# Attention of two transformer layers: score maxima in 512-key parts, the row of maxima by VectorE transposes, three or four score banks, and VectorE rounding four tiles per GQA head

## The reference, cut to what matters

```
def gqa_attend(q, k, v):
    s = jnp.einsum('bqhgd,bkhd->bhgqk', q, k).astype(jnp.float32) * (GQA_HEAD_DIM ** -0.5)
    p = jax.nn.softmax(s, axis=-1).astype(v.dtype)
    return jnp.einsum('bhgqk,bkhd->bqhgd', p, v)

def mla_attend(q_nope, q_rope, k_nope, k_rope, v):
    s = (jnp.einsum('bqhd,bkhd->bhqk', q_nope, k_nope)
         + jnp.einsum('bqhr,bkr->bhqk', q_rope, k_rope)).astype(jnp.float32) * ((MLA_NOPE + MLA_ROPE) ** -0.5)
    p = jax.nn.softmax(s, axis=-1).astype(v.dtype)
    return jnp.einsum('bhqk,bkhd->bqhd', p, v)
```

## Time and profile before

| | us |
|---|---|
| three runs | 3592.72, 3584.24, 3588.08 |
| median | 3588.08 |
| the profiled execution | 3586.85 |
| its span in the trace | 3585.0 |
| PE busy in it | 3351.6 (93%) |
| DVE, ACT, POOL busy | 2186.5, 1793.4, 1535.2 |
| GQA attention | about 1820 to 2382 |
| MLA attention | about 2919 to 3487 |

### The profile page before, as it was taken

The page is one execution under the profiler, slowest core; times in us unless marked ns, Lnnn a source line. Parts: engine busy times, 40 slices in busy tenths (PEclk is TensorE's granted clock), DMA queues, the critical chain, the costliest instruction groups (busy, mean ns, idle before and its releaser), DMA issues.

```text
span 3585.0 us, 47856 instructions
## 1 busy us (share of the span) xinstructions
PE 3351.6 (93%) x14934; PEld 2655.1 (74%) x14934; DVE 2186.5 (61%) x2655; ACT 1793.4 (50%) x3060; POOL 1535.2 (43%) x977
## 2 busy tenths in 40 slices
PE   7999999999999999799889999989888989999999
PEld 5777877778888887587777777767765667777767
DVE  6674877477575757447246666666558865555551
ACT  3343868242010101434158888861465657887870
POOL 3303444434444444510156666656210026666652
PEclk9999999999999999899999999999999989999999
DMA  2134232311212121123433443412254344332311
GB/s 99 53 117 119 75 77 81 119 41 66 75 59 88 55 86 35 58 102 115 124 89 66 102 85 76 103 64 89 97 197 149 118 118 111 65 82 53 76 42 71
DMA packets 196086, 313.52 MB, mean 87 GB/s; under 512 B 100928, under 2 KB 111680, under 8 KB 195968
## 3 DMA queue, kind: packets, MB, share of 16 engines
q1 hardware_dynamic: 195968, 312.01, 29.8%
HBM read 234.02 MB, written 77.92 MB: 87 GB/s over the span
## 4 chain that ended last, share of the span: by engine, by line
PE 68%; DVE 12%; issue 7%; ACT 6%; POOL 3%; DMA 2%; SPq 2%; DVEq 0%; ACTq 0%; POOLq 0%
PE PBX L281 10%; PE PBX L283 10%; PE PBX L282 10%; PE PMX L281 5%; PE PMX L282 5%; PE PMX L283 5%; PE PMX L1952 4%; PE PD L1993 2%; PE PD L1994 2%; PE PD L1995 2%; PE PD L856 2%; DVE gqa_m L2083 1%; PE PBX L1977 1%; PE PBX L1976 1%; PE PBX L1978 1%
## 5 line engine op out<-in xcount | busy, mean ns | idle before, releaser
L216 POOL TENSOR_TENSOR w_hi<-w_stage,zero 128x1024 fp32r<-128x1024 f32 (+2 forms) x123 | 229.1, 1863 | 1263.4 <-PE PBX L283 789.3
L2061 POOL TENSOR_TENSOR gqa_pl<-gqa_pf,gqa_ph 128x512 fp32r<-128x512 f32 (+1 forms) x288 | 370.9, 1305 | 186.3 <-ACT gqa_ph L2034 185.7
L2061 POOL TENSOR_TENSOR mla_pl<-mla_pf,mla_ph 128x512 fp32r<-128x512 f32 x256 | 351.8, 1383 | 206.9 <-ACT mla_ph L2034 202.7
L2083 DVE TENSOR_REDUCE gqa_m<-PMX 128x1 f32<-128x1280 f32 (+1 forms) x158 | 200.9, 1271 | 173.6 <-PE PMX L1952 172.7
L218 POOL TENSOR_TENSOR w_lo<-w_stage,w_hi 128x1024 fp32r<-128x1024 f32 (+2 forms) x123 | 299.9, 2438 | 9.7
L1678 ACT ACTIVATE conv_in<-PBX 128x512 f32<-128x512 f32 x66 | 39.6, 601 | 480.6 <-PE PBX L283 476.6
L2083 DVE TENSOR_REDUCE mla_m<-PMX 128x1 f32<-128x1280 f32 x126 | 187.3, 1487 | 89.5 <-PE PMX L1952 88.9
L2029 ACT ACTIVATE mla_pf<-PBX 128x512 f32<-128x512 f32 x320 | 190.1, 594 | 98.0 <-PE PBX L1978 88.1
L2029 ACT ACTIVATE gqa_pf<-PBX 128x512 f32<-128x512 f32 (+1 forms) x352 | 202.1, 574 | 52.8 <-PE PBX L1981 48.6
L2034 ACT ACTIVATE gqa_ph<-gqa_pf 128x512 fp32r<-128x512 f32 (+1 forms) x352 | 215.6, 612 | 13.8
L281 PE MATMUL PBX<-ffn_hi,w_hi 128*128 128x512 f32 x528 | 207.5, 393 | 8.5 <-DVE ffn_lo L653 8.5
(11 more groups left out here) (411 smaller groups left out, 9915.1 us busy)
## 6 DMA issues: line engine op xcount, KB each, us to landing
mod_w<-in_w_mod SPq DMA_DIRECT2D x48, 512.0 KB, 3.5
w_stage<-in_w_up SPq DMA_DIRECT2D x44, 512.0 KB, 3.4
w_stage<-in_w_go SPq DMA_DIRECT2D x24, 512.0 KB, 3.8
gqa_k<-kh_d SPq DMA_DIRECT2D x32, 320.0 KB, 4.9
gqa_q<-qh_d SPq DMA_DIRECT2D x32, 320.0 KB, 7.7
w_stage<-in_w_down SPq DMA_DIRECT2D x24, 384.0 KB, 3.0
qh_d<-heads_qh SPq DMA_DIRECT2D x32, 256.0 KB, 2.0
ql_d<-heads_ql SPq DMA_DIRECT2D x32, 256.0 KB, 2.3
```

Of the source, the lines that this page charges most:

```text
L216: pool.tensor_tensor(w_hi[s][:, 0:st.cols], w_stage[s][:, 0:st.cols], z, ALU.add).then_inc(w_hi_done, 1)
L2061: eng.tensor_tensor(self.PL[k % 4][:, 0:n], self.PF[k % 4][:, 0:n], self.PH[k % 4][:, 0:n].bitcast(F32), ALU.subtract).then_inc(self.lo_dv ...
L2083: dve.tensor_reduce(self.M[g % 2][:, t:t + 1], MX[:, 0:w], AX.X, ALU.max, negate=True)\
```

## The change

All of it is in `Attention`.

- Maxima are made in parts of at most 512 keys: three parts (512, 512, 256) for each tile, each in one bank, in two banks in turn. DVE reduces each part by itself into `m`, a table of 4 tiles by 3 parts.
- The row is made by DVE alone: a reduction over the parts with the sign turned, into column 0 of each 32 of `neg`, four 32 by 32 block transposes into `row`, and a copy of one row into Q. `diag`, `bcast` and ACT's row copy go.
- Score banks: three in GQA, four in MLA, for two. `pf`, `ph` and `pl` have rings of six (GQA) and five (MLA), for four. Three output banks in GQA, one per chunk, for two.
- `LAG` is 4, for 3; on DVE `final` stands two further steps behind.
- The two key blocks of a context chunk share one bank and are one step, so a GQA head has 21 steps.
- In the four GQA steps whose subtraction is DVE's, DVE also rounds `pf` to `ph`, which ACT did.
- The plan: parts go one to a step and two to a step in turn, and the next head's first maxima stand in step 11 of a GQA head and in step 10 of an MLA head. The first tile of chunk 1 is made in the head before.

```
-            LAG = 3
+            LAG = 4
-                self.S = [PB[0], PB[1]]
-                self.BC = PB[2]
-                self.O = [PD[0], PD[1]]
+                self.S = [PB[0], PB[1], PB[2]] + [PMX[:, 2 * C:3 * C]] * self.mla
+                self.NS, self.NP = len(self.S), len(self.PF)
+                self.O = [PD[0], PD[1], PMX[:, 2 * C:3 * C]][:len(chunks)]
+                self.MX = [PMX[:, 0:C], PMX[:, C:2 * C]]
+                self.groups = [[(t,) for t in keys[c]] if len(keys[c]) > 2 else [tuple(keys[c])]
+                               for c in range(len(chunks))]
...
                 else:
-                    plan += [(12 + 2 * t, "max", (1, 0), t) for t in range(4)] + [(21, "bcast", (1, 0), 0)]
+                    plan += [u for t in range(4) for u in tile((11 + 2 * t, 12 + 2 * t, 12 + 2 * t), (1, 0), t)]
+                    plan += tile((19, 20, 20), (1, 1), 0)
+                self.dve_hi = lambda k: not self.mla and self.dve_lo(k)
...
     (sp)
-                    sp.wait_ge(self.pv, i * self.SB + CR_PV2)
+                    sp.wait_ge(self.pv, i * self.SB + self.NP)
...
     (pe)
+                    lo, hi = self.part_keys(c, part)
+                    pe.matmul(MX[unit % len(MX)][:, 0:hi - lo], self.Q[q][0][0:mr, o:o + P], self.K[q][0][0:mr, lo:hi],
+                              start=True, stop=True).then_inc(self.max, 1)
-                    pe.matmul(self.BC[:, 0:n], ones[:, :], self.D[g % 2][:, 0:n // P, :], start=True, stop=True)\
-                      .then_inc(self.bcast, 1)
...
     (act)
-                    act.activation(dst, self.BC[r:r + 1, 0:n], ACT.Copy).then_inc(self.row_done, 1)
+                    if self.dve_hi(k):
+                        return
...
     (low)
+                if self.dve_hi(k):
+                    eng.wait_ge(self.pv, i * self.SB + (k + 1))
+                    eng.wait_ge(self.exp, i * self.SB + (k + self.NS + 1))
+                    eng.tensor_copy(self.PH[k % self.NP][:, :], self.PF[k % self.NP][:, :]).then_inc(self.hi_dve, 1)
...
     (dve)
+                    dve.tensor_reduce(NEG[:, 0:m, 0], M[:, 0:m, 0:parts], AX.X, ALU.max, negate=True).then_inc(self.neg, 1)
+                    for b in range(4):
+                        dve.transpose(blocks[:, :, b, :], NEG[32 * b:32 * b + 32, 0:m, :]).then_inc(self.turned, 1)
+                    dve.tensor_copy(self.Q[q][0 if self.mla else 1][r:r + 1, o:o + n], self.ROW[r:r + 1, 0:n])                       .then_inc(self.row_done, 1)
```

More of the change, by code:

```diff
@@ L1821, in __init__, with tile @@
+                self.steps = [(q, c, g, x == 0, x == len(self.groups[c]) - 1) for q in range(2)
+                              for c in range(len(chunks)) for x, g in enumerate(self.groups[c])]
                 self.SB = len(self.steps)
                 self.NC = len(chunks)
+                def tile(steps, at, t):
+                    return [(steps[p], at, t, p) for p in range(3)]
                 if self.mla:
-                    plan = [(2 * t, "max", (0, 1), t) for t in range(4)] + [(8, "bcast", (0, 1), 0)]
@@ new lines, in __init__ @@
+                    plan += [u for t in range(4) for u in tile((10 + 2 * t, 11 + 2 * t, 11 + 2 * t), (1, 0), t)]
+                    plan += tile((18, 19, 19), (1, 1), 0)
+                else:
+                    plan = [u for t in range(1, 4) for u in tile((2 * t - 2, 2 * t - 1, 2 * t - 1), (0, 1), t)]
+                    plan += [(7 + t, (0, 2), t, 0) for t in range(2)]
+                    plan += [u for t in range(4) for u in tile((11 + 2 * t, 12 + 2 * t, 12 + 2 * t), (1, 0), t)]
+                    plan += tile((19, 20, 20), (1, 1), 0)
@@ L1982, in scores @@
                     mm.then_inc(self.scores, 1)
                 def values(i, k):
-                    q, c, t, first, last_ = self.steps[k]
+                    q, c, tiles, first, last_ = self.steps[k]
                     n = self.chunks[c][1]
@@ L2045, in rden @@
+                    act.activation(rd, self.O[c][64:128, 0:n], ACT.Ln).then_inc(self.rden, 1)
                     act.wait_ge(self.rden, i * (4 * NC) + (2 * x + 1))
-                    act.activation(self.RD[:, 0:n], self.RD[:, 0:n], ACT.Exp, scale=-1.0).then_inc(self.rden, 1)
-                row(0, 0, 0, 0)
-                def step(i, k, last):
-                    for kind, q, c, t, g, tile, over in self.tasks(k, last):
-                        if kind == "bcast":
-                            row(i, q, c, g)
-                    probs(i, k)
@@ L2055, in act @@
-                self.run(act, step, lambda i, k: rden(i, k) if self.steps[k][4] else None)
-            def low(self, eng, i, k):
-                n = self.chunks[self.steps[k][1]][1]
-                eng.wait_ge(self.hi, i * self.SB + (k + 1))
-                eng.tensor_tensor(self.PL[k % 4][:, 0:n], self.PF[k % 4][:, 0:n], self.PH[k % 4][:, 0:n].bitcast(F32),
+                    act.activation(rd, rd, ACT.Exp, scale=-1.0).then_inc(self.rden, 1)
+                self.run(act, lambda i, k, last: probs(i, k), lambda i, k: rden(i, k) if self.steps[k][4] else None)
@@ L2086, in diag @@
[L2086 to L2093 removed]
+                dve.memset(self.NEG[:, :, :], 0.0).then_inc(self.neg, 1)
```

224 lines of the change are left out of this document (109 added, 115 removed).

## The result

| | before | changed |
|---|---|---|
| median | 3586.35 | 3751.54 |
| range of the runs | 3584.24 to 3592.72 | 3741.12 to 3756.14 |
| span of the profiled execution | 3585.0 | 3747.4 |
| granted clock of PE, mean | 0.977 | 0.957 |

The ratio is 1.0453, 95% interval 1.0427 to 1.048. The forecast was 3675, range 3600 to 3722: the right sign, the right first cause, and about half the size (+ 89 us for + 165); the time lies above the range.

The account below looks back on a forecast made before the run. Each head was taken as bound by its DMA load plus PE's work after it. With VectorE waits and low clock, GQA added 58.6 us and MLA 30.8; with the ends + 87, giving 3675 us, range 3600 to 3722.

Parts of the forecast that it names:

- Load arc: Last `values` to next head's first maxima: load 14.8 us GQA, 12.0 MLA; PE work beside it 9.0, so waits 5.8, 3.0.
- the two arcs: Each head is a circle: the load, then PE's work from first maxima to last `values`, 20.5 us GQA, 23.8 MLA.
- The 8 us: Formula estimate for a 2.62 MB GQA load, which would make the rival that loads do not bind true; chance 0.10.
- PE's work, ScalarE's waits: Per head, PE's work falls to 29.5 us in GQA and 32.8 in MLA; waits for ScalarE go.
- VectorE in the second arc: After the first maxima, PE waits for row making, rounding and `final`: 2.0 us per GQA head, 0.5 per MLA head.
- The clock: Behind each head's load wait PE runs at 1.2 GHz, losing 1.6 us per GQA head, 0.8 per MLA head.
- The rule that I set beside the sum: Each wait for a DMA is followed by the low clock, so MLA too pays 1.6 us, 10 us more in all.
- The sum: GQA head 38.9 us, MLA head 37.1; 13 periods each add 58.6 and 30.8 us.
- the ends: Outside the 13 periods: last arcs 3 us shorter in GQA, 1 in MLA; first rows 1 us later in each stage.
- VectorE too: Rival: dear transposes, rounding held up beside POOL, two low-clock stretches per wait; GQA 42, MLA 38.9, 3737 us; chance 0.18.
- dear transposes: In VectorE's row making, the rival's transposes cost the dear end, at most 0.42 us each; the forecast took 0.29.

Follow-up runs that it names:

- e6: The changed kernel, with PE making 20 (GQA) or 10 (MLA) matmuls that nobody reads while it would stand for the head's DMA: 3715.4 us.
- e10: e8 with VectorE subtracting half as many tiles and GpSimd taking the others: 3537.1 us, ratio 0.9858.
- e12: e10 with the changed kernel's load in one piece again: 3704.4 us, ratio 1.0334.
- e7: The changed kernel with the load split (first maxima wait only for what they read) and the row copied into Q by ScalarE: 3563.3 us.
- e8: e7 with ScalarE also rounding all tiles: 3562.1 us, ratio 0.9931.
- e9: The changed kernel, load in one piece, with the row copied into Q by ScalarE in place of VectorE: 3726.3 us, ratio 1.0386.
- e4: The changed kernel with ScalarE rounding all tiles again, none on VectorE: 3738.5 us, ratio 1.0411.
- e11: e2 with VectorE's row copy into Q written as a reduction over an axis of one element: 3641.9 us, ratio 1.016.
- e2: The changed kernel with the load split: first maxima wait only for the DMAs they read, first scores for the rest: 3657.0 us.

## Why the prediction was half right

- **Load arc.** Right. The load takes the 14.8 us forecast; DMA waits 5.6 and 3.1 for 5.8 and 3.0. e6 kept the load and lost only the clock; e10 and e12 differ in the load alone, and its price follows the two arcs. The 8 us that the prediction worked out from the Trainium skill's formula ("DMA: Bandwidth & Descriptors", Anatomy of one DMA) takes eight DMAs for one: the page gives 2.0 us plus bytes / 436 GB/s for each DMA.
- **PE's work, ScalarE's waits.** Right: 29.6 and 32.8 us, and no wait for ScalarE. But ScalarE had room for more: in e7, e8 and e9, where it copies the row, PE waits only 0.5 us per GQA head for it, in e10 not at all, and e8, where it does all the rounding too, is among the fast ones.
- **VectorE in the second arc.** The failed step. 2.0 and 0.5 us were forecast; PE's waits there are 3.05 and 1.3, and with the small gaps behind them about 3.4 and 1.7. The places are where I put them. Means over the 13 GQA heads:

| wait for VectorE | forecast | changed | e4, no rounding | e9, no copy |
|---|---|---|---|---|
| step 17 | 0.9 | 0.89 | 0.24 | 0.89 |
| step 20 | 0.9 | 1.13 | 1.13 | 0.68 |
| step 0 | 0.7 | 1.03 | 0.57 | 0.33 |
| sum | 2.5, taken as 2.0 | 3.05 | 1.94 | 1.90 |

The fourth wait, 0.49 at step 7, stands in the load's arc and costs nothing there. Half a microsecond of the miss is the deduction from 2.5 to 2.0 ("since back-to-back DVE instructions overlap"), which the waits don't show. The other half is in steps 20 and 0. VectorE's and PE's rows of one head, with GpSimd's at 2192.39 (1.28 us) as above:

```profile
2167.12 1.20 DVE L2101 CAST gqa_q<-gqa_row 1x512 fp32r<-1x512 f32 x1
...
2187.06 0.50 PE L1965 MATMUL PMX<-gqa_k,gqa_q 128*128 128x512 f32 x1 [0.67 <-DVE gqa_m L2083]
...
2192.85 1.10 DVE L2057 CAST gqa_ph<-gqa_pf 128x512 fp32r<-128x512 f32 x1
2192.87 0.38 PE L1965 MATMUL PMX<-gqa_k,gqa_q 128*128 128x256 f32 x1 [1.02 <-DVE gqa_m L2083]
...
2195.33 0.50 PE L1965 MATMUL PMX<-gqa_k,gqa_q 128*128 128x512 f32 x1 [0.83 <-DVE gqa_m L2083]
```

Up to step 20 the chain went as forecast: 3.8 us from the first reduction to the last, with transposes of 0.30 and a copy of 0.42; it began 0.2 us late. Behind it the rounding, taken as "CAST 0.427", started beside GpSimd and took 1.06 to 1.19 in all 13 heads. The subtraction behind it took 0.69, less than the 0.84 forecast, so about 0.5 more stands ahead of step 0. The dear copies of e11's rows are not the cause in GQA: all 13 of 1.20 to 1.43, and the smaller ones of the context chunk (0.62 to 0.73), stand in the load's arc, as at 2167.12. They bind only once the load is split, in the pile of e2.

In MLA a held instruction stands ahead of both waits. One head:

```profile
3372.56 1.49 DVE L2114 TENSOR_TENSOR MIX<-MIX,mla_gate 64x512 f32 x1
...
3377.26 1.55 DVE L2101 CAST mla_q<-mla_row 1x512 fp32r<-1x512 f32 x1
```

```profile
3377.25 1.28 POOL L2061 TENSOR_TENSOR mla_pl<-mla_pf,mla_ph 128x512 fp32r<-128x512 f32 x1 [0.80 <-ACT mla_ph L2033]
```

```profile
3379.59 0.39 PE L1965 MATMUL PMX<-mla_k,mla_q 96*128 96x256 f32 x1 [1.22 <-DVE mla_m L2083]
```

At step 19 PE waits 1.4 us in five of the 13 heads, the five whose copy took 1.55 to 1.57; in the other eight the copy took 0.42 and there is no wait, and with the copy on ScalarE (e9) there is none in any. At step 17 it waits 0.76 in all 13, behind a gate product of 1.48 to 1.49 that takes 0.69 beside an idle GpSimd; no run takes this hold-up away, so that part is argued. What failed, then, is that I took the rounding, the copy and `final` from places where GpSimd stood idle. The row for `final`, 0.68, was that of the product that reads PSUM, which took 0.67 to 0.69 beside GpSimd too. The mean of 0.84 for the subtraction in the earlier trace rows held the warning: 39 of 52 took 0.69 and the 13 that started beside a busy GpSimd about 1.25.
- **The clock.** The term for GQA was near (1.9 for 1.6). For MLA I took half of the stretch in the earlier trace rows, since no row showed a wait of 3 us in a steady stretch; it is 1.7 for 0.8. The rule that I set beside the sum, the Trainium skill's HAM oscillation ("TensorE: Matmul & The Clock Gate"), holds for MLA too: each of the 13 heads waits for its DMA and goes on at the low level, and e6 shows the cause.
- **The sum.** Per head the forecast misses 2.3 us in each stage, 26 x 2.3 = 60 of the 75 us that the span misses. The rest is in the ends, where I counted -2 and the profile has +13: the two last arcs were to be 3 and 1 us shorter and are 5.0 longer and unchanged, and the two first heads were to come 1 us later each and come 5.1 and 3.8 later. Which terms make these stays open.
- **The rival "VectorE too"** (3737) was the nearest. Of its causes, dear transposes did not happen, and the rounding held up beside POOL did, in one of its three places per head (13 of 39 took 1.06 to 1.19).
- **What no step had.** Two bounds stand one behind the other in GQA. With the load in one piece, relieving VectorE as in e12 gives 47 us; splitting the load alone gives 94; both give 214, or 73 more than the sum of the two. Whoever had removed either alone would have found the change still slower than before.

Left open: why four GQA heads of e6 fall to the low clock behind the same three waits that leave the others at full speed, and what makes the ends.

## What to carry to other kernels

When a change takes PE's work away from beside a transfer of fixed length, count what the transfer still covers, and who else was hiding in its shadow: the second bound shows only when the first is gone. Wait for the bytes that the next instruction reads, not for the whole load. Price a VectorE instruction that copies within SBUF or reads two operands there at both ends, with GpSimd idle and with GpSimd busy, and in the stretch that binds, and give small copies on the critical chain to ScalarE or to a form that is slower but steady.

## What the runs showed of the hardware

- A VectorE copy of one row of 512 from SBUF to SBUF took 0.42 us in each of the 13 GQA cases (1871 to 2406) with GpSimd idle at its start, and 1.20 to 1.43 in each of the 13 with GpSimd busy; the held copies end 0.28 us behind GpSimd's instruction. The same copy as a reduction over one element: 0.68 in all cases. In MLA, where the copy started first, the GpSimd subtraction took about 1.5 in place of 1.28.
- After waits of 2.5 to 3.7 us in every MLA head TensorE ran at a granted clock of 0.50 to 0.76 for the next 3.4 us; with the wait filled by matmuls that nobody reads, the stage ran at 1.00.
- A block transposition on VectorE takes 0.30 us for 32 x 128 and 0.24 for 32 x 64, one started each 0.33 and 0.27.
- Of a load of 2.62 MB that takes 14.8 us in one piece, the four DMAs that the first maxima need, issued first, land within 8.1 to 8.8 us of the first issue: no wait in 13 heads.
